# Seven modulation column groups as weighted sums under the first feed forward, softmax factors spread by GpSimd, and turns placed inside the last projection of the odd block

## The reference, cut to what matters

```python
for i in range(DEPTH):
    ml = jnp.split(s_lat @ w_ada[i] + b_ada[i], 6, axis=-1)
    mc = jnp.split(s_ctx @ w_ada[i] + b_ada[i], 6, axis=-1)
    u_lat = modulate(h_lat, g_pre_mix[i], ml[0], ml[1])
    ...
    h_lat = h_lat + ml[2] * rms_norm_2(o_lat, g_post_mix[i])
    f_lat = sqrelu_mlp(modulate(h_lat, g_pre_ff[i], ml[3], ml[4]), w_ff1[i], w_ff2[i])
    h_lat = h_lat + ml[5] * rms_norm_2(f_lat, g_post_ff[i])
```

## Time and profile before

| what | value |
|---|---|
| median of 3 executions | 1934.95 us (1932.95 to 1937.16) |
| the profiled execution | 1936.78 us, its span 1934.9 us |
| mean granted PE clock | 0.995 of full speed |
| PE busy | 1869.8 us, 97% of the span |
| DVE busy | 1105.8 us, 57% |
| ACT busy | 861.6 us, 45% |
| POOL busy | 211.9 us, 11% |
| 16 DMA engines, mean busy share over the stretches 832 to 875 / 1190 to 1540 us | 0.61 / 0.32 |

### The profile page before, as it was taken

One profiled execution on the slowest core, in us unless ns is written; L12 is line 12 of the kernel. 1 busy time (PEld: TensorE's weight loads), 2 busy tenths in 40 slices (PEclk: granted clock), 3 DMA queues, 4 the chain that ended last, 5 costly groups with the idle time before them and its releaser, 6 DMA issues. The chain is left out here.

```text
span 1934.9 us, 37112 instructions
## 1 busy us (share of the span) xinstructions
PE 1869.8 (97%) x15824; PEld 1559.3 (81%) x15824; DVE 1105.8 (57%) x1835; ACT 861.6 (45%) x1559; POOL 211.9 (11%) x249
## 2 busy tenths in 40 slices
PE   7999999999999999999999999999999999899998
PEld 5768998776899788756898888888887798579986
DVE  6566774566667554476557665444444565546643
ACT  5465653446656542465322335322222254655532
POOL 2101221110122100103122211000000011000000
PEclk9999999999999999999999999999999999899999
DMA  7777665467766541353000042333332234024653
GB/s 267 250 256 224 189 183 175 166 227 263 223 166 195 175 142 55 115 174 110 26 4 4 4 151 65 104 119 98 100 107 88 66 99 139 25 88 133 194 180 124
DMA packets 219354, 264.68 MB, mean 137 GB/s; under 512 B 14214, under 2 KB 153782, under 8 KB 214711
## 3 DMA queue, kind: packets, MB, share of 16 engines
q1 hardware_dynamic: 218603, 261.49, 42.4%
q10 hardware_dynamic: 588, 0.82, 0.1%
HBM read 261.20 MB, written 1.09 MB: 136 GB/s over the span
## 5 line engine op out<-in xcount | busy, mean ns | idle before, releaser
L404 PE MATMUL acc<-rounded,rounded 128*128 128x512 f32 (+1 forms) x2552 | 875.1, 343 | 9.6 <-DVE rounded L684 4.1
L405 PE MATMUL acc<-rounded,rounded 128*128 128x512 f32 (+1 forms) x2552 | 867.0, 340 | 0.0
L406 PE MATMUL acc<-rounded,rounded 128*128 128x512 f32 (+1 forms) x2552 | 866.8, 340 | 0.0
L388 DVE TENSOR_TENSOR rounded<-arena,rounded 128x2048 fp32r<-128x2048 f32 (+1 forms) x194 | 434.3, 2241 | 285.9 <-ACT rounded L377 285.8
L404 PEld LDWEIGHTS acc<-rounded,rounded 128*128 128x128 f32 x2552 | 480.6, 188 | 80.1 <-issue 14.7
L405 PEld LDWEIGHTS acc<-rounded,rounded 128*128 128x128 f32 x2552 | 480.7, 188 | 60.0 <-issue 1.9
L406 PEld LDWEIGHTS acc<-rounded,rounded 128*128 128x128 f32 x2552 | 480.5, 188 | 60.0
L377 ACT ACTIVATE rounded<-arena 128x2048 fp32r<-128x2048 f32 (+1 forms) x194 | 362.9, 1873 | 341.6 <-PE acc L406 296.4
L1624 DVE SCALAR_TENSOR_TENSOR arena<-acc,pcol,arena 128x254 f32<-128x254 f32 (+1 forms) x176 | 76.8, 478 | 52.3 <-ACT arena L1605 50.8
L2200 PE MATMUL sc<-arena 64*64 64x64 f32 x2560 | 94.7, 221 | 8.8 <-DVE arena L2350 7.7
L2764 ACT ACTIVATE arena<-acc 128x512 f32<-128x512 f32 (+1 forms) x64 | 31.4, 490 | 159.6 <-PE acc L406 159.6
(11 more groups left out here) (265 smaller groups left out, 1691.6 us busy)
## 6 DMA issues: line engine op xcount, KB each, us to landing
arena<-in_w_ff SPq DMA_DIRECT2D x64, 1024.0 KB, 5.4
arena<-in_w_ada SPq DMA_DIRECT2D x48, 1024.0 KB, 5.1
arena<-in_w_up SPq DMA_DIRECT2D x88, 512.0 KB, 5.1
arena<-in_w_in SPq DMA_DIRECT2D x24, 1024.0 KB, 5.3
arena<-in_w_down SPq DMA_DIRECT2D x20, 1024.0 KB, 5.0
arena<-in_w_out SPq DMA_DIRECT2D x16, 1024.0 KB, 5.1
arena<-in_w_in_even SPq DMA_DIRECT2D x9, 1024.0 KB, 5.3
arena<-in_w_in_odd SPq DMA_DIRECT2D x8, 1024.0 KB, 5.2
```

The source lines that it names most:

```text
L388: dve.tensor_tensor(r32(w), w, r32(high_slot(c)[:, 0:size(c)]), ALU.subtract).then_inc(split_made, 1)
L404: pe.matmul(ps, ah, bh, start=first, stop=False)
L405: pe.matmul(ps, ah, bl, start=False, stop=False)
L406: return pe.matmul(ps, al, bh, start=False, stop=last)
```

## The change

Groups 16 to 22 leave the even block's attentions; only group 23 stays, under units 0 and 1 of attBl. The seven groups become 14 unsplit chunks ("late"), put into the chunk list ahead of each `ff1` but the first and each `ff2` but the last. DVE multiplies each by the condition, four 128 x 512 steps per chunk, accumulating in one buffer `late_sum`; `late_pe` sums over the partitions with four small products per group inside `ff2`; `late_add` adds the bias. The gates of the odd block get a turn of their own after the projection's first part, and SP stores them just ahead of the last output projection's first chunk.

The factor 1/sum is spread along the free axis by a POOL copy (`widen`, 128 x 128, 48 of them) and PE turns the copy with one turn in place of two products. The POOL products `kka` of the recurrence's preparation are put between these copies.

`decays_dve` moves from attBl to the DVE program of the projection before it; `kd_dve` starts at unit 0. In `proj1_pe` the D tiles 0 and 1 are turned ahead of the third token tile of `proj1_v`, 2 and 3 ahead of the fourth, 4 and 5 behind it, and ACT copies them in the same order.

The core of the diff:

```diff
+        def plan_late():
+
+            n = len(late_chunk)
+            view = I["w_ada_2"][1].rearrange("(k p) n -> p k n", p=P)
+            c, k0 = 512 * (4 + n // 2), 4 * (n % 2)
+            late_chunk.append(len(chunks))
+            whole.add(len(chunks))
+            chunks.append(view[:, k0:k0 + 4, c:c + 512])
+            release.append((late_read, n + 1))
+            if n % 2:
+                stage(("late", n // 2), tr=1)
...
+                late_dve(dve, c)
...
-        stage("attBl", acc=16, tr=16 + 4, sc=8 + 4)
-        plan_ada(range(16, 20), lambda n: sc_at["attBl"] + 3 * n)
-        stage("attBc", acc=16, tr=8 + 4 + 8, sc=8 + 4)
-        plan_ada(range(20, 24), lambda n: sc_at["attBc"] + 3 * n)
+        stage("attBl", acc=16, tr=16 + 1, sc=8 + 1)
+        plan_ada([23], lambda n: sc_at["attBl"])
+        stage("attBc", acc=16, tr=8 + 8, sc=8)
...
         def plan_ff1(e):
+            if e:
+                plan_late()
...
         def plan_ff2(e):
+            if e < EIGHTHS - 1:
+                plan_late()
...
-                pe.wait_ge(att_comb, self.base + u + 1)
-                for m in range(2):
-                    ins = pe.matmul(ps[m * HD:(m + 1) * HD, P:2 * P], self.recip[:, 2 * u + m:2 * u + m + 1].broadcast_to([P, HD]), ident,
-                                    start=True, stop=True, tile_position=(0, m * HD))
+                i = self.featured.index(u)
+                pe.wait_ge(att_wide, self.spread_units + i + 1)
+                ins = pe.transpose(ps[:, P:2 * P], self.wide[:, i % 2, :], ident)
                 ins.then_inc(POOLS[self.values_at(u)[0]][1], 1)
...
+            def widen(self, pool, before=None):
+
+                for i, u in enumerate(self.featured):
+                    if before and u in before:
+                        before[u]()
+                    pool.wait_ge(att_comb, self.base + u + 1)
+                    if i >= 2:
+                        pool.wait_ge(att_spread, self.spread_units + i - 1)
+                    pool.tensor_copy(self.wide[:, i % 2, :].rearrange("p (m e) -> p m e", m=2),
+                                     self.recip[:, 2 * u:2 * u + 2].unsqueeze(2).broadcast_to([P, 2, HD])).then_inc(att_wide, 1)
...
+        def late_dve(dve, c):
+
+            while late_done[0] < len(late_chunk) and late_chunk[late_done[0]] + 2 <= c:
+                n = late_done[0]
+                late_done[0] += 1
+                if n and n % 2 == 0:
+                    late_add(dve, n // 2 - 1)
+                g = late_chunk[n]
+                wait_landed(dve, g)
+                if n % 2:
+                    dve.wait_ge(late_read, n)
+                w = shaped(raw_slot(g), g)
+                for k in range(4):
+                    s = silu_c[:, 4 * (n % 2) + k, 0:1]
+                    if n % 2 == 0 and k == 0:
+                        ins = dve.tensor_scalar(late_sum, w[:, k, :], s, None, ALU.mult)
+                    else:
+                        ins = dve.scalar_tensor_tensor(late_sum, w[:, k, :], s, late_sum, ALU.mult, ALU.add)
+                    if k < 3:
+                        link(dve, ins)
+                ins.then_inc(late_read, 1)
+
+        def late_pe(pe, b):
+
+            pe.wait_ge(late_read, 2 * b + 2)
+            ps = claim(pe, "tr", tr_at[("late", b)])
+            for n in range(4):
+                ins = pe.matmul(ps[:, 2 * n:2 * n + 2], late_sum[:, n * P:(n + 1) * P], ones[:, 0:2], start=True, stop=True)
+            ins.then_inc(tr_full, 1)
...
+        def late_gains(dve):
+
+            wait_drained(dve, "tr", tr_at[("late", EIGHTHS - 2)])
+            wait_drained(dve, "tr", att_bl.ada_tr[0])
+            pre_gain(dve, 1, 1)
+            for w in range(2):
+                post_gate(dve, 1, w).then_inc(mod_ready, 1)
...
+            for d in range(2):
+                decays_dve(dve, d)
...
-                if u < 2:
-                    decays_dve(dve, u)
-                else:
-                    kd_dve(dve, *divmod(u - 2, 4))
+                if u < 8:
+                    kd_dve(dve, *divmod(u, 4))
...
+            att.widen(pool, {1: key_rates((0, 0)), 2: key_rates((0, 1)), 3: key_rates((0, 2)), 4: key_rates((0, 3), (1, 0)),
+                             5: key_rates((1, 1), (1, 2)), 6: key_rates((1, 3))})
...
-                ada_gains(dve, att_bc.ada_tr[-1], 1)
+                wait_drained(dve, "tr", tr_at[("group_turn", 3)])
+                pre_gain(dve, 1, 0).then_inc(mod_ready, 1)
...
+                late_add(dve, EIGHTHS - 2)
...
+                    if block == 1 and n == 0:
+                        late_pe(pe, key[1])
...
+            pe.wait_ge(mod_ready, 5)
+            pe.transpose(claim(pe, "tr", tr_at["late_gates"])[0:2 * KT * 2, 0:P], gates_of[1], ident).then_inc(tr_full, 1)
...
-            tok_gemm(pe, "proj1_v", PV, KT, [ALL], token_tile)
-            for n, (x, f, nh, c, lat) in enumerate(D_UNITS):
+
+            def turn_unit(n):
+                x, f, nh, c, lat = D_UNITS[n]
                 pe.wait_ge(d_normed, n + 1)
                 ps = claim(pe, "tr", tr_at["proj1"] + n)
                 for j in range(nh // 2):
                     ins = pe.transpose(ps[:, j * P:(j + 1) * P], x[:, j * P:(j + 1) * P], ident)
                 ins.then_inc(tr_full, 1)
 
+            def among(block, k0, n):
+                if k0 and n >= 2:
+                    for i in (2 * n - 4, 2 * n - 3):
+                        turn_unit(i)
+
+            tok_gemm(pe, "proj1_v", PV, KT, [ALL], token_tile, before=among)
+            for n in (4, 5):
+                turn_unit(n)
...
+                    if tt in (1, 2):
+                        for n in (2 * tt - 2, 2 * tt - 1):
+                            keep_unit(n)
+                for n in (4, 5):
+                    keep_unit(n)
...
+                    wait_drained(sp, "tr", tr_at["late_gates"])
+                    mix1.gate_out(sp)
+                    ff1.gate_out(sp)
...
+            att_bl.widen(pool)
```

More of the change, by code:

```diff
@@ L511, in first_and_second_block @@
         plan_norm(("mix", 1, 0))
+        stage("late_gates", tr=1)
         stage("proj1", acc=4 + 4 + 4 + 2 + 4, tr=6)
@@ L816, in __init__ @@
                 self.ada = list(ada) if ada is not None else []
-                self.sc = [sc_at[key] + u + (u // 2 + 1 if self.ada else 0) for u in range(n)]
+                self.sc = [sc_at[key] + u + min(u // 2 + 1, len(self.ada)) for u in range(n)]
                 self.base = att_units[0]
@@ L833, in __init__ @@
                 for u in range(n + 1):
[L834 removed]
+                    if u % 2 == 0 and 2 <= u <= 2 * len(self.ada):
                         self.ada_tr.append(f)
@@ L1240, in first_and_second_block, with late_add @@
         mod_ready = sem("mod_ready")
-        mod_gates = mod_gate.rearrange("p l w k s -> p (l w k s)")
+        gates_of = [mod_gate[:, l].rearrange("p w k s -> p (w k s)") for l in range(DEPTH)]
+        late_done = [0]
+        def late_dve(dve, c):
[24 more added lines that the diff above has]
+            ins.then_inc(tr_full, 1)
+        def late_add(dve, b):
+            f = tr_at[("late", b)]
+            ps = filled(dve, "tr", f)
+            dve.tensor_tensor(mod[:, 1, 16 + 4 * b:20 + 4 * b, :], ps[:, 0:8].rearrange("p (a b) -> p a b", a=4),
+                              col("b_ada_2", 6 * KT + 16 + 4 * b, 4).unsqueeze(2).broadcast_to([P, 4, 2]), ALU.add)\
+               .then_inc(drain("tr", f), 1)
         def ada_pe(pe, att, i, n):
@@ L1732, in first_and_second_block @@
         at_ff0_end = r4.at
+        late_sum = Region(at_ff0_end + 9 * SEQ).take(512)
         r4 = Region(at1)
@@ L2077, in prep_pool, with key_rates, place @@
             pool.wait_ge(prep_done, 8)
-            for d in range(2):
-                for j in range(4):
-                    wait_drained(pool, "tr", att.more[3 if d else j])
-                    pool.tensor_tensor(kka[d][:, j, :], kk[:, j, :], rates[d][:, j, :], ALU.mult).then_inc(kka_done, 1)
+            def key_rates(*pairs):
+                def place():
+                    for d, j in pairs:
+                        wait_drained(pool, "tr", att.more[3 if d else j])
+                        pool.tensor_tensor(kka[d][:, j, :], kk[:, j, :], rates[d][:, j, :], ALU.mult).then_inc(kka_done, 1)
+                return place
+            att.widen(pool, {1: key_rates((0, 0)), 2: key_rates((0, 1)), 3: key_rates((0, 2)), 4: key_rates((0, 3), (1, 0)),
+                             5: key_rates((1, 1), (1, 2)), 6: key_rates((1, 3))})
             for d in range(2):
@@ L2877, in first_and_second_block @@
         spread2 = Region(at_y2).take(2, P)
+        wide2 = Region(at_y2 + 2 * P).take(2, P)
         yT2 = uT1
@@ L3142, in _ @@
                     wait_drained(sp, "tr", tr_at["gates"])
-                    for post in posts.values():
-                        post.gate_out(sp)
+                    mix0.gate_out(sp)
+                    ff0.gate_out(sp)
                 if g == chunk_at["out2_0"] + 1:
```

97 lines of the change are left out of this document (54 added, 43 removed).

## The result

The changed kernel takes **1926.99 us** (median of 4 executions, 1925.38 to 1927.88), the kernel before beside it 1936.06 us (1932.95 to 1937.29). The ratio is 0.9950 with a 95% interval of 0.9935 to 0.9964: 9.1 us faster where 19.6 were forecast, and 1 us above the range of 1906 to 1926. The profiled execution has a span of 1924.9 us for 1934.9.

What follows compares the result with a forecast made beforehand. PE, busy 97%, was taken as the bound in attBl, attBc and the first feed forward. Terms -8.4 - 11.6 - 5.5 + 6.7 - 0.8 = -19.6 took the profiled 1936.8 to 1917.2, median 1915.4 us; range 1906 to 1926.

Steps and rivals of the forecast that it cites:

- Copies and turn, -5.5: All attentions: spreading 1/sum by POOL copy and one turn saves 0.19 us in 32 units; -5.5 us, bounds -6.5 and -2.
- attBl, -8.4: Attention stage attBl: without the groups DVE sets the pace, 34.0 us against 42.4, -8.4.
- five units of 3.64 us: Within the attBl sum: five units at DVE's own pace of 3.64 us, 18.2 us.
- My upper bound: In attBl: if the chain adds 0.3 us per unit, the stage takes 2 us more.
- attBc, -11.6: Attention stage attBc: 2.85 us a unit, set by the chain through all engines; 25.7 us against 37.3, -11.6.
- port lock: Rival, attBl and attBc: POOL copies hold up DVE through the shared ports, 6.4 us, giving 1921.8; chance 0.12.
- First feed forward, +6.7: First feed forward: PE gains seven times 0.95 us of late products, all showing; +6.7 us, 6.4 to 8.
- Odd projection, -0.8: End of the odd projection: earlier turns gain little, since DVE's split then delays the maxima; -0.8 us, -2.5 to +0.5.
- Half clock in part: Rival, attBl and attBc: idle PE gets the lower clock for a third of both, giving 1925; chance 0.06.
- Shorter chains: Rival: PE's own sums set the pace, 3 us less in attBl and 2.5 in attBc, giving 1910; chance 0.12.
- not what it says: Rival: attention units stay as long because another chain already has their length, giving 1935.4; chance 0.04.
- starved splits: Rival, first feed forward: the 4.4 us margin is gone, PE waits 1.3 us at 14 places, giving 1934; chance 0.05.

Runs made afterwards that it cites:

- e12: e9 with the denominators spread by two products of 64 columns, without POOL's copies, POOL's key products held at the same units: 1920.21 us, ratio 0.9923.
- e3: Changed kernel plus eight products on constants on PE ahead of attC's third scores, in its wait: 1922.77 us, ratio 0.9944.
- e4: Changed kernel with one product of 8 columns for four of 2 per late group, three quarters of its modulation uncomputed: 1919.90 us, ratio 0.9925.
- e7: Changed kernel with DVE's half of the split of an out2_1 chunk moved behind attC's third unit: 1926.09 us, ratio 0.9949.
- e6: Changed kernel with three of eight kd_dve calls taken out of attBl's units ahead of its last maxima: 1925.79 us, ratio 0.9952.
- e9: Changed kernel with kd_dve calls moved, constant products in PE's waits at the joints, and DVE's out2_1 split in attC's tail: 1917.62 us, ratio 0.9905.
- e1: Changed kernel with the denominators spread by two products of 64 columns again in all 48 units, no POOL copies: 1928.51 us, ratio 0.9972.
- e11: e9 with the third and fourth near product of the first such round, and DVE's additions, moved to the round's second half: 1915.66 us, ratio 0.9895.
- e2: Changed kernel with the six turns of the D units and their ACT copies behind the last tile again: 1924.77 us, ratio 0.9953.
- e8: Changed kernel with constant products in PE's longer waits: even block, recurrence's first level, attC's and attD's third scores: 1922.25 us, ratio 0.9932.

## Why the prediction was wrong, step by step

**Copies and turn, -5.5: the term was mis-sized.** It was 32 units of 0.32 - 0.13. The 0.13 came from a turn inside a row of eight. In its real place the turn's rows of the changed kernel are, in attC:

```profile
1655.76 1.09 PE L919 MATMUL sc<-arena 128*64 128x128 f32 x16
1656.78 0.33 PE L923 MATMUL sc<-keep,arena 128*128 128x128 f32 x1
1656.95 1.04 PE L896 MATMUL tr<-keep,arena 128*128 128x128 f32 x8
```

Values to spread is 1.02 us, before it was 0.92; spread to tiles is 0.17. PE goes from 128*64 to 128*128 tiles once in either kernel. Before, that was inside the 0.32 us that I counted as removable. The Trainium skill (TensorEngine Tiling (Array Packing), "Key Properties") says that a change of tiling mode drains TensorE; the extra 0.10 us agrees with it. So 1.24 became 1.19, with 0.05 more in the tiles behind: 0.10 us a unit, not 0.19. In the first attentions it was less. From first scores to last values they fell from 34.22 to 33.77 and from 36.69 to 36.24 us, 0.45 each for 8 units, and from the first scores of the first to attBl 0.6 us are left, of the 3 forecast. (The table's -0.3 hides half of it behind a start that was 0.27 us later, ahead of all attentions.) The 1.6 us of the joint C/D went with the clock: before, it was 0.66 of full speed there from 1685 to 1690, and the joint is 8.61 in e12 too, with products but PE kept busy. Whether the copies have a part in where such an episode falls isn't shown: unfilled, both kernels with products had one, and two of the seven with the turn.

**attBl, -8.4: mechanism right, size off.** It gave -4.8; where the clock stayed up (e3, e4, e7) -6.3 (35.97). The step that was mis-sized is the five units of 3.64 us. The unit of 3.64 is there, but only every second one. DVE's rows of the changed kernel:

```profile
853.54 0.29 DVE L1031 COPY arena<-sc 128x128 f32<-128x128 f32 x1
...
857.65 0.29 DVE L1031 COPY arena<-sc 128x128 f32<-128x128 f32 x1 [0.47 <-PE sc L923]
...
861.26 0.29 DVE L1031 COPY arena<-sc 128x128 f32<-128x128 f32 x1
...
866.39 0.29 DVE L1031 COPY arena<-sc 128x128 f32<-128x128 f32 x1 [2.86 <-PE sc L923]
```

Units last 4.1 and 3.6 us in turn: a unit that DVE does at its own pace hands PE its tile late, and DVE waits 0.47 us in the next. My upper bound had 0.3 for that, and I took none. e6 and e9 show DVE's part: with its calls moved attBl is 34.90 and 33.69 (e9 keeps PE busy as well). The profiled execution lost 1.5 us more to a lower clock behind two waits (of 1.39 and 1.88 us, PE):

```profile
859.87 1.09 PE L919 MATMUL sc<-arena 128*64 128x128 f32 x16 [1.39 <-ACT arena L1092]
...
863.97 1.98 PE L919 MATMUL sc<-arena 128*64 128x128 f32 x16 [1.88 <-ACT arena L1092]
...
866.15 1.64 PE L896 MATMUL tr<-keep,arena 128*128 128x128 f32 x8
```

`decays_dve` cost nothing, as forecast: 4.59 us of idle were left behind it, by the prediction 4.7.

**attBc, -11.6: right.** It was -11.4 where the clock stayed up, -10.3 in the profiled execution. The price of 2.85 us a unit holds (values start 2.4 to 3.5 us apart, 2.9 in the mean). The **port lock** is there and is small: a 128 x 2 step of DVE that begins 0.1 us after a key product of POOL lasts 1.19 us, until that product ends. It was 0.66 before, where it began later in the product, and 0.16 at 872.31 us, with no product beside it. Beside the products six of the eight such steps are long (0.66 to 1.19 us), two of them by 0.5 us more than before; a copy takes 0.29 us and can't hold one that long (POOL's rows, then DVE's):

```profile
887.65 2.50 POOL L2171 TENSOR_TENSOR arena<-arena 128x512 f32<-128x512 f32 x2
890.10 0.29 POOL L1021 COPY pcol<-stat 128x128 f32<-128x128 f32 x1
```

```profile
887.75 1.19 DVE L969 TENSOR_TENSOR stat<-stat,neg_sink 128x2 f32<-128x2 f32 x1
```

The Trainium skill's rule on the shared ports (SBUF - State Buffer, "SBUF: two separate sides"), that whoever starts first holds them for its whole instruction, agrees with this row; that the lock would cost 6.4 us here by the copies was wrong, e1 and e12 being slower, not faster, without the copies.

**First feed forward, +6.7: it was +7.65.** The products are right (seven times 0.9, e4). The step that was left out is that DVE's order was followed for the splits only; the near addition, behind split and late steps, was the later one (1.15 us, gone in e11). Splits never starved PE. Their loads landed later, though. The view of ACT's split L392 shows what ended its waits, with their total and number; this releaser had 3.0 us, once, before:

```profile
  DMA arena<-in_w_ff: 85.0, 19
```

**Odd projection, -0.8: it was +0.9, the right worry with a term left out.** The first maxima came 5.4 us behind the last product instead of 8.4 (my times give 5.8), and DVE's split was ahead of them as I said (1638.52 us, 2.29). Counted from the last near product they came 1.7 us earlier, where I had 0.8. What I left out is what PE does meanwhile: it waited 4.21 us and then did 6 us of work at the lower clock (2.5 us, e3), so the first spread came 0.9 us later. I had the clock as a bound of this term and as a rival for the even block only.

**Rivals.** Half clock in part is what happened, but in episodes of some us at the joints (two in the profiled execution: 864 to 878 and 1638 to 1650 us) instead of through a third of both stages. Its 1925 lies nearest to the measured time by luck: the clock took 2.6 us of the even block, and the rest of the miss is in other terms. Such episodes stood in the rows before (0.57 and 0.69). I counted the clock as a thing that the change might bring, and not as one that can come at any joint where PE then waits. Shorter chains and "not what it says" are out; starved splits are out, though their loads came later.

**The missing sum.** Of 9.6 us between forecast and profiled spans, 3.6 were missing in attBl (1.5 of them clock), 1.3 in attBc (1.1 clock), 0.95 in the feed forward, 1.7 at the odd projection (clock), and 2.0 in the rest, where the forecast had 5.5 for the copies. What the copies brought outside the even block is 2.3 us of 5.5 (0.6 in the first attentions, 1.5 in attC and attD, 0.3 behind), so their own miss was 3.2; the joint's 1.6 of clock covered half of it, by luck.

## What to carry to other kernels

Price an instruction by the distance of starts in the place where it will stand: a switch of tile shape belongs to whoever comes next, and isn't saved by removing one of the two. Where PE work is taken off ahead of a joint, ask what PE does in the time won, since part of it comes back as slow work behind the new wait, and move the work that holds up the next engine (here DVE's split of 2.3 us) to where its engine waits anyway. And compare stage lengths over several kernels that share the code before a microsecond is put down to an edit, and count from a mark inside the stage: a start that moved by 0.3 us hid half of what the first attentions gained.

## What the runs showed of the hardware

- PE's granted clock went to its lower level (1.2 for 2.4 GHz) behind short waits: behind 1.39 and 1.88 us with work between them, and behind 1.51 us in the recurrence. Behind equal waits it stayed up in other executions (1.50 us in the changed kernel). The joint C/D has the same wait of 1.54 us in nine kernels: in five the work behind it ran at full clock (8.62 us), in three it slowed from the turn on (10.2: before, e1 and e7), in one at once (11.84, e6, with the very code of the changed kernel there). With PE kept busy in that wait it was 8.62 in five of five. Products on constants in the waits of attC's start kept the clock at 1.00.
- Stretches of untouched code differed between executions: the start up to the first attention's scores by 1.9 us (96.4 to 98.2), the second of the first attentions by 1.5 (36.24, and 37.7 in e2, e8 and e11, at a clock of 0.83 from 436 to 446 us), the recurrence by 2.2 (3.6 with e1), the joint C/D by 3.2 (8.62 to 11.84). The joint and the attention go with the clock, the recurrence only by 0.9 us of it. The rest stays open.
